# Four places of a two-block transformer kernel: the split of the mixed tiles, the feed-forward norm, the order of the pools, and the rope keys of the first head

## The reference, cut to what matters

```python
# first block, end of the mixer and start of the feed-forward
x = x + jnp.einsum("bsd,de->bse", g_a * y_a + g_b * y_b, w_o[i])
h = rmsnorm(x, g_ffn[i])
u = jnp.einsum("bsd,df->bsf", h, w_up[i])
f_gate = causal_dwconv(u[..., :D_FF], conv_f_w[i]) + conv_f_b[i]
...
# second block: pools over windows of 2, 4, 8 and 16 tokens, one group of 128 columns each
pooled = (win_sum / cnt - ug.astype(jnp.float32)).astype(u.dtype)
y = jnp.einsum('blgc,gcd->blgd', pooled, w_pool).reshape(B, L, D_POOL)
...
br_p = jax.nn.silu(gate_p) * _multiscale_pool(pool_in, w_pool, pool_scale)
# second block: 4 heads of attention over 1280 keys; a key is 128 columns of its own and 64 rotated ones, common to all heads
k = jnp.concatenate(
    [k_nope, jnp.broadcast_to(k_rope[:, :, None, :], (B, L, MLA_HEADS, QK_ROPE_DIM))], axis=-1)
q = _rms(q, q_norm_g)
k = _rms(k, k_norm_g)
```

## Time and profile before

| | us |
|---|---|
| median of three runs | 2145.03 |
| lowest, highest | 2144.63, 2150.13 |
| the profiled execution | 2146.71 |
| its span, first to last instruction | 2144.8 |
| mean granted TensorE clock | 0.978 of full |
| busy in the span: PE, DVE, ACT, POOL | 2058.4, 1179.1, 439.1, 731.1 |

### The profile page before, as it was taken

One profiled execution on the slowest core, in us unless ns is written; L12 is line 12 of the kernel. 1 busy time (PEld: TensorE's weight loads), 2 busy tenths in 40 slices (PEclk: granted clock), 3 DMA queues, 4 the chain that ended last, 5 costly groups with the idle time before them and its releaser, 6 DMA issues.

```text
span 2144.8 us, 24911 instructions
## 1 busy us (share of the span) xinstructions
PE 2058.4 (96%) x9765; PEld 1711.7 (80%) x9765; DVE 1179.1 (55%) x1119; ACT 439.1 (20%) x547; POOL 731.1 (34%) x534
## 2 busy tenths in 40 slices
PE   6999999999998999999999999999899989999998
PEld 5888788887876888888888888878788778888877
DVE  4999994213435755665556655744433735556520
ACT  4000002201221000000000000233212235555411
POOL 2444464444322333333333334423123411112221
PEclk9999999999998999999999999999799989999999
DMA  4111111231131122211222112211122210000033
GB/s 139 53 49 49 30 54 45 70 102 54 40 120 30 43 74 79 62 56 44 73 78 67 50 44 73 79 30 40 30 95 73 78 36 1 11 11 1 1 128 89
DMA packets 176850, 122.07 MB, mean 57 GB/s; under 512 B 8771, under 2 KB 160272, under 8 KB 176784
## 3 DMA queue, kind: packets, MB, share of 16 engines
q1 hardware_dynamic: 175504, 118.77, 18.4%
q10 hardware_dynamic: 1280, 2.35, 0.3%
HBM read 112.71 MB, written 8.39 MB: 56 GB/s over the span
## 4 chain that ended last, share of the span: by engine, by line
PE 82%; DVE 6%; issue 3%; POOL 3%; DMA 3%; ACT 2%; SPq 0%; DVEq 0%; POOLq 0%; ACTq 0%
PE ps L488 69%; DMA raw<-in_w_up 2%; POOL wlo L437 2%; PE ps L864 2%; DVE prob L1851 1%; POOL whi L435 1%; PE ps L897 1%; PE ps L899 1%; PE ps L878 1%; PE ps L898 1%; PE ps L881 1%; PE ps L875 1%; PE ps L872 1%; PE ps L547 1%; PE ps L884 1%
## 5 line engine op out<-in xcount | busy, mean ns | idle before, releaser
L437 POOL TENSOR_TENSOR wlo<-raw,whi 128x1024 fp32r<-128x1024 f32 (+2 forms) x162 | 459.2, 2835 | 13.5
L434 POOL TENSOR_TENSOR small<-ones 128x1 f32<-128x1 f32 x166 | 52.4, 316 | 1143.6 <-PE ps L488 947.7
L488 PE MATMUL ps<-xb_hi,whi 128*128 128x512 f32 x1216 | 383.4, 397 | 24.8 <-DVE xb_lo L1595 4.3
L488 PE MATMUL ps<-xa_hi,whi 128*128 128x512 f32 x1184 | 373.7, 395 | 7.9 <-DVE xa_lo L1586 3.6
L488 PE MATMUL ps<-xb_lo,whi 128*128 128x512 f32 x1216 | 379.0, 393 | 0.0
L488 PE MATMUL ps<-xb_hi,wlo 128*128 128x512 f32 x1216 | 378.0, 392 | 0.0
L488 PE MATMUL ps<-xa_lo,whi 128*128 128x512 f32 x1184 | 369.2, 391 | 0.0
L488 PE MATMUL ps<-xa_hi,wlo 128*128 128x512 f32 x1184 | 368.7, 391 | 0.0
L488 PEld LDWEIGHTS ps<-xb_hi,whi 128*128 128x128 f32 x1216 | 228.8, 190 | 81.8 <-issue 8.6
L488 PEld LDWEIGHTS ps<-xb_lo,whi 128*128 128x128 f32 x1216 | 231.2, 190 | 49.4
L488 PEld LDWEIGHTS ps<-xb_hi,wlo 128*128 128x128 f32 x1216 | 230.8, 190 | 49.1
(11 more groups left out here) (325 smaller groups left out, 2250.2 us busy)
## 6 DMA issues: line engine op xcount, KB each, us to landing
raw<-in_w_in SPq DMA_DIRECT2D x52, 512.0 KB, 3.8
raw<-in_w_up SPq DMA_DIRECT2D x44, 512.0 KB, 4.1
raw<-in_w_down SPq DMA_DIRECT2D x22, 512.0 KB, 3.5
w_mod<-in_w_mod SPq DMA_DIRECT2D x40, 256.0 KB, 3.3
x_columns<-in_x SPq DMA_DIRECT2D x8, 512.0 KB, 5.0
raw<-in_w_o SPq DMA_DIRECT2D x8, 512.0 KB, 3.8
raw<-in_w_ple_gate SPq DMA_DIRECT2D x8, 512.0 KB, 3.9
y_scratch<-resid SPq DMA_DIRECT2D x8, 512.0 KB, 3.0
```

The lines of the kernel that those rows point to most:

```text
L434: nc.gpsimd.tensor_tensor(small[:, 106 + slab.slot:107 + slab.slot], ones[:, 0:1], ones[:, 0:1], ALU.mult)
L437: nc.gpsimd.tensor_tensor(lo, src, f32(hi), ALU.subtract).then_inc(split_done, 1)
L488: ins = mm(dst[j], w, r[j], start=first and f, stop=last and l)
```

## The change

**Mixed tiles.** DVE makes the low parts of tiles 0 to 2 ahead of the multiplication of tile 7, and ACT's first copy waits for one job less (for the last gate product, which still reads the old tiles).

**Feed-forward norm.** The first up product takes each tile as it comes. The column sums stand within it ahead of k tile 6, the broadcast within the second ahead of k tile 4. On ACT and DVE the norm's chain is put ahead of the context's, which gets other small columns.

**Pools.** The groups go in the order 16, 8, 4, 2. The reciprocal chain of the query norm moves from behind the first group into it, behind its second add. The gate's SiLU tile gets its own place.

**Rope keys.** The high and low parts of the rotated keys move into the first head: two copies on ACT behind the squares of the keys, the low part on DVE behind the rope query's multiplications, the third copy behind a query's square. `csq` gets its own place, so that SP loads it once the last gate product is done. Of the two bank pairs, PE waits for the second only ahead of the third key product. The latent tiles move by 1024 bytes, and SP loads the pool slabs in the new order of groups (neither is shown).

```diff
+GROUPS = (3, 2, 1, 0)
...
-    sgp = at("silu_gate_p", [P, S], F32, o_t + 5120)
+    sgp = at("silu_gate_p", [P, S], F32, o_t + 9216)
...
-    csq = at("cos_sin_q", [P, S], F32, o_r + 26624)
+    csq = at("cos_sin_q", [P, S], F32, o_xbh + 62464)
...
-        sp.wait_ge(sem("kr_hi"), 2)
-        sp.wait_ge(sem("kr_lo"), 1)
+        sp.wait_ge(job_done, JOBS["pool"] + 7)
...
-        pe.wait_ge(sem("fx_lo"), 8)
-        for k in range(2):
-            gemm(J + k, L + k, XBh, XBl, KD, w8)
-        column_sums(rbc, 8, 0, sem("ss_done"), 9)
-        broadcast(T[3][:, 0:1024].rearrange("p (t n) -> p t n", n=P), 8, 2)
+        def up_sums(n):
+            if n == 6:
+                column_sums(rbc, 8, 0, sem("ss_done"), 9)
+        def up_scale(n):
+            if n == 4:
+                broadcast(T[3][:, 0:1024].rearrange("p (t n) -> p t n", n=P), 8, 2)
+        gemm(J, L, XBh, XBl, KD, w8, each_k=(sem("fx_lo"), 0), between=up_sums)
+        gemm(J + 1, L + 1, XBh, XBl, KD, w8, between=up_scale)
...
-        for gq in range(4):
-            gemm(J + 2 * gq, L + gq, XBh, XBl, KD, w8)
-            pe.wait_ge(sem("pool_lo"), gq + 1)
-            gemm(J + (2 * gq + 1), None, XAh[:, 4 + gq:5 + gq, :], XAl[:, 4 + gq:5 + gq, :], 1,
+        for n, gq in enumerate(GROUPS):
+            gemm(J + 2 * n, L + n, XBh, XBl, KD, w8)
+            pe.wait_ge(sem("pool_lo"), n + 1)
+            gemm(J + (2 * n + 1), None, XAh[:, 4 + gq:5 + gq, :], XAl[:, 4 + gq:5 + gq, :], 1,
...
-        for s in range(2):
-            pe.wait_ge(pair_free[s], JOBS["heads"] // 2)
+        pe.wait_ge(pair_free[0], JOBS["heads"] // 2)
...
                 turn(before, 1)
+            if h == 0:
+                pe.wait_ge(pair_free[1], JOBS["heads"] // 2)
             key_product(h, 2).then_inc(sem("kn_pe"), 1)
...
-                act.wait_ge(job_done, JOBS["wo"])
+                act.wait_ge(job_done, JOBS["wo"] - 1)
...
+        root(8, 2)
...
-        fn(sd[:, 0:2], var[:, 0:2], ACT.Sqrt).then_inc(sem("row_sd"), 1)
-        root(8, 2)
+        fn(sd[:, 8:10], var[:, 8:10], ACT.Sqrt).then_inc(sem("row_sd"), 1)
...
-        for gq in range(4):
-            J = Lin(JOBS["pin"] + gq)
-            if gq == 0:
+        def gate_silu(n):
+            J = Lin(JOBS["pool"] + 2 * n)
+            act.wait_ge(job_done, J.val(1))
+            if n >= 1:
+                act.wait_ge(sem("pool_ready"), 4 + n)
+            fn(sgp[:, :], pair(J), ACT.Silu).then_inc(*one(free(J)))
+        def pool_high(n):
+            act.wait_ge(sem("pool_ready"), n + 1)
+            fn(XAh[:, 4 + GROUPS[n % 4], :], pl[:, :], ACT.Copy).then_inc(sem("pool_hi"), 1)
+        for n, gq in enumerate(GROUPS):
+            J = Lin(JOBS["pin"] + n)
+            if n == 0:
...
-                act.wait_ge(sem("pool_ready"), gq)
+                act.wait_ge(sem("pool_ready"), n)
...
-            act.wait_ge(sem("pool_ready"), gq + 1)
-            if gq == 0:
+            if n == 0:
...
-            fn(XAh[:, 4 + gq, :], pl[:, :], ACT.Copy).then_inc(sem("pool_hi"), 1)
-            if gq == 0:
...
-        for gq in range(4):
-            J = Lin(JOBS["pool"] + 2 * gq)
-            act.wait_ge(job_done, J.val(1))
-            if gq >= 1:
-                act.wait_ge(sem("pool_ready"), 4 + gq)
-            fn(sgp[:, :], pair(J), ACT.Silu).then_inc(*one(free(J)))
-            act.wait_ge(sem("pool_ready"), 4 + gq + 1)
-            fn(XAh[:, 4 + gq, :], pl[:, :], ACT.Copy).then_inc(sem("pool_hi"), 1)
-        act.wait_ge(sem("pool_lo"), 8)
-        for v in range(2):
-            fn(KRs[ROPE * v:ROPE * (v + 1), :], krot[:, :], ACT.Copy).then_inc(sem("kr_hi"), 1)
-        act.wait_ge(sem("kr_lo"), 1)
-        fn(KRl[ROPE:P, :], f32(KRl[0:ROPE, :]), ACT.Copy).then_inc(sem("kr_lo"), 1)
+            pool_high(n)
+        for n in range(4):
+            gate_silu(n)
+            pool_high(4 + n)
...
                 turned_hi(before, 3)
+            else:
+                for v in range(2):
+                    fn(KRs[ROPE * v:ROPE * (v + 1), :], krot[:, :], ACT.Copy).then_inc(sem("kr_hi"), 1)
             act.wait_ge(sem("rope_pe"), h + 1)
...
             fn(sqk[:, 0:H], PS[:, 0:H], ACT.Square).then_inc(sem("qn_sq"), 1)
+            if h == 0:
+                act.wait_ge(sem("kr_lo"), 1)
+                fn(KRl[ROPE:P, :], f32(KRl[0:ROPE, :]), ACT.Copy).then_inc(sem("kr_lo"), 1)
             act.wait_ge(sem("nope_pe"), 2 * h + 2)
...
         mix("mix_b", 7, 8, False)
-        mix("mix_a", 0, 8, True)
+        mix("mix_a", 0, 7, True)
         for m in range(8):
+            if m == 3:
+                mix("mix_a", 7, 8, True)
             dve.wait_ge(sem("mx_hi"), m + 1)
...
+        rstd(8, D, 2, 2, 2, T[3][:, 0:1024].rearrange("p (t n) -> p t n", n=P))
...
-        ts(var[:, 0:2], c_ss[:, 0:2], 1.0 / D, EPS, ALU.mult, ALU.add).then_inc(sem("row_var"), 1)
+        ts(var[:, 8:10], c_ss[:, 0:2], 1.0 / D, EPS, ALU.mult, ALU.add).then_inc(sem("row_var"), 1)
...
-        nc.vector.reciprocal(rcp[:, 0:2], sd[:, 0:2]).then_inc(sem("row_rcp"), 1)
+        nc.vector.reciprocal(rcp[:, 8:10], sd[:, 8:10]).then_inc(sem("row_rcp"), 1)
...
-            ts(cstage[:, t, :], cstage[:, t, :], rcp[:, t:t + 1], None, ALU.mult).then_inc(sem("cs_ready"), 1)
+            ts(cstage[:, t, :], cstage[:, t, :], rcp[:, 8 + t:9 + t], None, ALU.mult).then_inc(sem("cs_ready"), 1)
...
-        rstd(8, D, 2, 2, 2, T[3][:, 0:1024].rearrange("p (t n) -> p t n", n=P))
...
+                if at_n == 0 and s == 1:
+                    rstd(8, 256, 6, 6, 5, at_col=16, to=rql)
...
-            dve.wait_ge(sem("inv_in"), 16 * (gq + 1))
-            if gq >= 1:
-                dve.wait_ge(sem("pool_lo"), gq)
...
+            dve.wait_ge(sem("inv_in"), 16 * (at_n + 1))
+            if at_n >= 1:
+                dve.wait_ge(sem("pool_lo"), at_n)
...
-            if gq == 0:
-                rstd(8, 256, 6, 6, 5, at_col=16, to=rql)
-        for gq in range(4):
-            J = Lin(JOBS["pool"] + 2 * gq)
+        for at_n, gq in enumerate(GROUPS):
+            J = Lin(JOBS["pool"] + 2 * at_n)
...
-            if gq == 0:
-                dve.wait_ge(sem("pool_lo"), 4)
-            else:
-                dve.wait_ge(sem("pool_lo"), 4 + gq)
+            dve.wait_ge(sem("pool_lo"), 4 + at_n)
...
-        dve.wait_ge(sem("kr_hi"), 2)
-        tt(KRl[0:ROPE, :], krot[:, :], f32(KRs[0:ROPE, :]), ALU.subtract).then_inc(sem("kr_lo"), 1)
...
             tt(PS[0:ROPE, 3 * H:5 * H], PS[0:ROPE, 3 * H:5 * H], csq[0:ROPE, :], ALU.mult).then_inc(sem("qr_a"), 1)
+            if h == 0:
+                dve.wait_ge(sem("kr_hi"), 2)
+                tt(KRl[0:ROPE, :], krot[:, :], f32(KRs[0:ROPE, :]), ALU.subtract).then_inc(sem("kr_lo"), 1)
             query_lo(0)
```

More of the change, by code:

```diff
@@ L377, in sync_program @@
                  A["w_pool_2"][0, 2 * u:2 * u + 2].rearrange("g p n -> p g n"))
-        for gq in range(4):
-            slab8(Lin(SLABS["pool"] + gq), w2, OFF_GP + gq * P)
+        for n, gq in enumerate(GROUPS):
+            slab8(Lin(SLABS["pool"] + n), w2, OFF_GP + gq * P)
         w_kv, w_q = A["w_ukv_2"][0], A["w_uq_2"][0]
@@ L1789, in vector_program @@
         n = [0]
-        for gq in range(4):
-            J = Lin(JOBS["pin"] + gq)
+        for at_n, gq in enumerate(GROUPS):
+            J = Lin(JOBS["pin"] + at_n)
             dve.wait_ge(*free(J))
@@ L1812, in vector_program @@
             tt(pl[:, :], src[:, a:a + S], inv[:, :], ALU.mult).then_inc(sem("pl_mul"), 1)
-            dve.wait_ge(sem("pl_mul"), gq + 1)
+            dve.wait_ge(sem("pl_mul"), at_n + 1)
             tt(pl[:, :], pl[:, :], upad[:, 8:8 + S], ALU.subtract).then_inc(sem("pool_ready"), 1)
-            dve.wait_ge(sem("pool_hi"), gq + 1)
+            dve.wait_ge(sem("pool_hi"), at_n + 1)
             tt(XAl[:, 4 + gq, :], pl[:, :], f32(XAh[:, 4 + gq, :]), ALU.subtract).then_inc(sem("pool_lo"), 1)
-            if gq == 0:
-                rstd(8, 256, 6, 6, 5, at_col=16, to=rql)
-        for gq in range(4):
-            J = Lin(JOBS["pool"] + 2 * gq)
+        for at_n, gq in enumerate(GROUPS):
+            J = Lin(JOBS["pool"] + 2 * at_n)
             dve.wait_ge(job_done, J.val(2))
             dve.wait_ge(*free(J))
-            if gq == 0:
-                dve.wait_ge(sem("pool_lo"), 4)
-            else:
-                dve.wait_ge(sem("pool_lo"), 4 + gq)
+            dve.wait_ge(sem("pool_lo"), 4 + at_n)
             stt(pl[:, :], pair(J + 1), col("pool_scale_2", gq), sgp[:, :], ALU.mult, ALU.mult).then_inc(sem("pool_ready"), 1)
             after_all(*one(free(J + 1)))
-            dve.wait_ge(sem("pool_hi"), 4 + gq + 1)
+            dve.wait_ge(sem("pool_hi"), 4 + at_n + 1)
             tt(XAl[:, 4 + gq, :], pl[:, :], f32(XAh[:, 4 + gq, :]), ALU.subtract).then_inc(sem("pool_lo"), 1)
```

15 lines of the change are left out of this document (7 added, 8 removed).

## The result

The changed kernel takes 2125.68 us in the median of four runs (2123.06 to 2126.19), the kernel before 2144.83 on the same chip (four runs, 2142.33 to 2150.13). The ratio is 0.9911 with an interval of 0.9896 to 0.9925: faster by 0.9%, 1.7 us over the forecast of 2124. Measured again later, it took 2124.02 in the median of five runs against 2147.23 (eleven runs), a ratio of 0.9895 (0.9877 to 0.9913). The profiled execution is the shortest of the first four, 2123.06 with a span of 2121.3.

What follows compares the result with a forecast made beforehand. PE, busy 96% of the span, was taken as the bound, so only its idling or lower clock could yield time. Gains 2.3 + 14.0 + 2.6 + 3.0 = 21.9 us gave 2124.8 or 2123.1, stated as 2124; range 2118 to 2133.

Steps and rivals of the forecast that it cites:

- Part A: Mixed tiles: low splits ahead of tile 7's multiplication let PE's second transposes start earlier; gain 2.3 us, bounds 0.5 and 3.4.
- the lower bound of 0.5: Mixed tiles: PE meets the fourth split late, idles and falls to the low clock inside the product; gain only 0.5 us.
- later than 16 us after the first: Mixed tiles, sign of a wrong prediction: PE's second transposes come later than 16 us after the first.
- Part B: Feed-forward norm inside the first up products: PE starts them at once, idles 1.2 at the broadcast; gain 14.0 us, bounds 6 and 15.2.
- Part C: Pools: with the window of 16 first, 0 to 2 us of PE's 3.5 SiLU wait stay; gain 2.6, bounds 1.0 and 3.5.
- Part D: First head: rope-key work moved into it, key products start earlier, scores at about 1770.7 instead of 1773.6; gain 3.0, bounds -2 and 6.
- PE idles 6.2: First head: the value products wait 6.2 us for the rope query's sum, which comes at 1763.5, and the clock falls again.
- (1): Rival, norm: its loads don't move, PE idles 5.6 in the second up product; gain there 6, time 2132.8 us; chance 0.10.
- (2): Rival, mixed tiles and pools: DVE and POOL block each other; gains there only 0.5 and 1.0, time 2128.2 us; chance 0.15.
- (3): Rival, first head: moved rope keys only move the wait and the clock stays low; -2 there, time 2129.8 us; chance 0.12.
- (4): Rival, first head: slower, as stop and go holds the clock at 1.2 GHz; until the second head, 2162 us; chance 0.03.
- (5): Rival, whole kernel: no change, what is saved is waited for again at later loads; 2145 us; chance 0.03.

## Why the prediction was right, and where not

The time, 2125.68, lies 1.7 from the forecast and inside the range; the sum of 21.9 compares with 22.5 by the stretches. It came out well partly because two errors cancel, A's (1.3 too much) and D's (1.5 too little), and the median has luck in it too: it moved by 19.2 us in one measurement and by 23.2 in the other, with the same two kernels.

- **Part A: 2.3 forecast, 1.0 in the profiled execution, 2.5 in the second.** DVE's chain ran as forecast. I had allowed 3.0 us for what the low splits lose while POOL splits; of that, the second part fell on the add instead. The step that failed is "PE itself could start at 520.3 and need 10.9, so this chain decides". PE needed 10.9 plus its idle 3.06, since only three tiles were ready. At full clock that ends as late as the chain; in five of the eight executions that have this code (A from 16.4 to 18.0; 15.1 to 15.2 in the other three) the clock fell inside the product. That was the mechanism of the lower bound of 0.5, and in the worst of them, 18.0, the edit gained nothing against 17.7. By my own mark, "later than 16 us after the first", this part was wrong in the profiled execution (16.7) and right in the second (15.2).
- **Part B: 14.0 forecast, 14.2 measured**, and 14.0 with this part alone. The idle time at the broadcast was put at 1.2 and is 0.96, broadcast and products followed at full clock, and the two later products filled the 22.0 us from 646.0 to 668.0 (24.8 before).
- **Part C: 2.6 forecast, 2.8 measured.** Of the SiLU wait 0.8 is left, within the "0 and 2 us". The last pooled tile came at 1703.1 in old positions (1662.04 + 41.0), within 1700 to 1704.
- **Part D: 3.0 forecast, 4.2 to the scores and 4.5 to the maxima.** The chain was right and 1.0 us too long: keys' squares and low parts went 0.6 to 0.8 faster than I put them. The value products start 15.9 after the last pool multiplication (16.9 forecast). The forecast "PE idles 6.2" failed: it idled 2.6. The clock had already fallen within the second query product, after an idle time of 1.07, so PE reached the wait 13.3 after that multiplication (10.8 forecast). In the second execution the clock fell only within the wait itself; PE reached it after 10.9 and idled 5.0, which is 6.2 less the 1.0 by which the chain was shorter and the 0.1 to 0.2 by which PE came later. D is the same 22.9 in both: the chain on ACT and DVE decides, not PE.
- **Rivals.** (1) The norm's loads did move, by 4.65 us. (2) The contention came in part A, as a mechanism: 3.45 beside POOL, 1.22 without it. The rule of the Trainium skill (SBUF — State Buffer, section Who interferes with whom), that a DVE instruction with at most one SBUF input does not contend with GpSimd, agrees in these rows: the multiplication, which reads PSUM and one SBUF tile, took 1.21 beside POOL's high part (522.48 to 523.53) and 1.21 with POOL at rest. What I made of it for the pools, C at 1.0, did not come: C gained 2.8. (3) and (4) did not come; the clock was back by 1755. (5) fell.

## What to carry to other kernels

A reduction and its broadcast can stand inside the products that they scale, if each is set ahead of the k tile that PE reaches just when its input is ready; then ask what stands ahead of the chain between them on its own engines, for that was worth a third of the gain (4.4 of 14.2), and one more move another 1.2. When work is moved off one wait, look at the next thing released behind its new place: here the sum for the value products, worth 2.7 us. And when DVE's adds of two SBUF tiles decide, look at what POOL does in the same microsecond: starting POOL's split later gave 2.2 to 3.8 us against the two executions of the changed kernel, where the edit on DVE gave from nothing to 2.6 over eight.
